# A two-layer hybrid attention trunk in fp32: the sparse values and their gate computed by channel instead of by token

## What is computed

```python
h = rms_norm(x, pre_w)
dq, dk, dv, dg, sq, sk, sv, sg, iq, ik, iw = split(h @ w_in)
oa = diff_attention(dq, dk, dv)              # 4 heads, value dim 128
oa = rms_norm(oa, subln_w) * (1 - lambda_init) * silu(dg)
score = relu(iq @ ik) . iw                   # index scores, 8 heads
idx = top_k(score, 64)                       # the 64 keys of each query
ob = softmax(sq @ sk[idx]) @ sv[idx]         # 4 heads of dim 128
ob = ob * silu(sg)
x = x + rms_norm(concat(oa, ob) @ w_out, post_w)
```

## Time and profile before

| | |
|---|---|
| median of 3 runs | 299.26 us |
| time of the profiled execution | 298.92 us |
| its span | 297.1 us |
| granted TensorE clock, mean | 0.996 |
| busy: PE / DVE / ACT / POOL | 97% / 79% / 55% / 25% |
| DMA: read, written | 56.06 MB, 6.82 MB |

### The profile page before, as it was taken

How to read it: one execution, slowest core, us unless ns; L and a number is a source line. 1 busy time by engine, 2 the same in 40 slices (tenths; PEclk the granted TensorE clock), 3 DMA queues, 4 the chain that set the end, 5 groups by cost and what they waited for, 6 DMA issues and landing times.

```text
span 297.1 us, 4373 instructions
## 1 busy us (share of the span) xinstructions
PE 289.3 (97%) x1544; PEld 243.8 (82%) x1544; DVE 234.4 (79%) x474; ACT 164.4 (55%) x284; POOL 74.9 (25%) x116
## 2 busy tenths in 40 slices
PE   8999999999999999899999999999999999999992
PEld 7799877788877888788888988778887788888892
DVE  4755789898978999867984686968898799999343
ACT  6988664635366775503676764473742948651101
POOL 6559410303305133001061740003302140210101
PEclk9999999999999999999999999999999999999998
DMA  7999959558755948994049796947768297476012
GB/s 251 369 365 394 387 214 317 195 130 251 189 194 91 336 143 216 225 290 138 1 146 377 236 358 144 393 164 195 231 128 284 47 272 262 142 137 147 0 71 71
DMA packets 77173, 63.15 MB, mean 213 GB/s; under 512 B 47200, under 2 KB 54112, under 8 KB 77152
## 3 DMA queue, kind: packets, MB, share of 16 engines
q1 hardware_dynamic: 76864, 62.62, 68.2%
q10 hardware_dynamic: 288, 0.26, 0.3%
HBM read 56.06 MB, written 6.82 MB: 212 GB/s over the span
## 4 chain that ended last, share of the span: by engine, by line
PE 85%; DVE 6%; DMA 3%; ACT 3%; issue 1%; SPq 1%; POOLq 0%; DVEq 0%; POOL 0%; ACTq 0%
PE bank_a L474 17%; PE bank_a L479 17%; PE bank_a L483 17%; PE bank_a L631 7%; PE bank_s L631 6%; PE bank_a L491 4%; PE bank_o L608 3%; ACT xt_pbuf L845 2%; DVE w_lo L1001 2%; PE bank_t L453 2%; DMA pT<-turned 1%; PE bank_s L572 1%; DMA turned<-dkT 1%; PE bank_o L757 1%; PE bank_s L584 1%
## 5 line engine op out<-in xcount | busy, mean ns | idle before, releaser
L1001 DVE TENSOR_TENSOR w_lo<-w_raw,w_hi 128x2048 fp32r<-128x2048 f32 (+1 forms) x46 | 99.4, 2168 | 17.2 <-ACT w_hi L774 16.9
L774 ACT ACTIVATE w_hi<-w_raw 128x2048 fp32r<-128x2048 f32 (+1 forms) x46 | 81.9, 1785 | 28.4 <-PE bank_a L483 19.7
L474 PE MATMUL bank_a<-w_hi,h_hi 128*128 128x512 f32 (+1 forms) x272 | 72.1, 387 | 0.0
L479 PE MATMUL bank_a<-w_hi,h_lo 128*128 128x512 f32 (+1 forms) x272 | 69.9, 378 | 0.0
L483 PE MATMUL bank_a<-w_lo,h_hi 128*128 128x512 f32 (+1 forms) x272 | 69.8, 378 | 0.0
L479 PEld LDWEIGHTS bank_a<-w_hi,h_lo 128*128 128x128 f32 x272 | 49.8, 188 | 9.6
L483 PEld LDWEIGHTS bank_a<-w_lo,h_hi 128*128 128x128 f32 x272 | 49.8, 188 | 9.5
L474 PEld LDWEIGHTS bank_a<-w_hi,h_hi 128*128 128x128 f32 x272 | 48.1, 188 | 10.5 <-issue 2.7
L1444 POOL TENSOR_TENSOR rt<-nat,tab 128x256 f32<-128x256 f32 x10 | 8.5, 854 | 103.6 <-ACT nat L829 103.6
L829 ACT ACTIVATE nat<-bank_a,st 128x512 f32<-128x512 f32 x20 | 13.6, 686 | 30.7 <-PE bank_a L483 30.7
L845 ACT ACTIVATE xt_pbuf<-xt_pbuf,st 128x128 f32<-128x128 f32 (+1 forms) x48 | 21.2, 443 | 14.5 <-DVE st L1150 14.5
(11 more groups left out here) (198 smaller groups left out, 426.3 us busy)
## 6 DMA issues: line engine op xcount, KB each, us to landing
w_raw<-in_w_in SPq DMA_DIRECT2D x30, 1024.0 KB, 6.6
w_raw<-in_w_out SPq DMA_DIRECT2D x8, 1024.0 KB, 5.7
w_raw<-in_w_in SPq DMA_DIRECT2D x8, 584.0 KB, 7.5
turned<-mixn SPq DMA_DIRECT2D x28, 128.0 KB, 2.7
prm<-in_rows SPq DMA_DIRECT2D x2, 705.0 KB, 7.7
w_raw<-in_w_in SPq DMA_DIRECT2D x2, 512.0 KB, 6.0
xres<-in_x SPq DMA_DIRECT2D x2, 512.0 KB, 9.4
dqT<-turned SPq DMA_DIRECT2D x2, 512.0 KB, 5.9
```

The source lines that it names most:

```text
L474: pe.matmul(bank, h_hi[:, HALF * half + kk, tok], whi[:, kk, :], start=half == 0 and kk == 0, stop=False)
L479: pe.matmul(bank, h_lo[:, HALF * half + kk, tok], whi[:, kk, :], start=False, stop=False)
L774: act.activation(unit(w_hi, u), unit(raw, u), ACT.Copy).then_inc(hi_done.sem, 1)
L1001: dve.tensor_tensor(unit(w_lo, u), unit(raw, u), unit(w_hi, u).bitcast(F32), ALU.subtract).then_inc(lo_done.sem, 1)
```

## The change

- **Gate (chunk SG).** `turned_gate` swaps the operands: a 128x128 tile of weights is stationary, the moving operand is `h` over all 256 tokens. A group is now two tiles of 128 channels by 256 tokens, 48 matmuls of 256 columns instead of 24 of 512. The gate stands by channel, and each token is a column.
- **Root per column.** `rx` can no longer be ACT's per-partition scale. SP writes it to DRAM (before unit 9's DMA) and reads it back as a row on all partitions (`rx_rows`, before unit 11's DMA). ACT's move is a plain copy. POOL multiplies the gate by `rx_rows` in two instructions of 128x512 ahead of the DQ rotary embedding, and ACT applies Silu in place, two instructions of 128x512 after split_hi(13).
- **Probabilities.** DVE's reciprocals move ahead (`invert(12)`, `invert(13)`, `invert(14)`), POOL multiplies the exponentials by 1/sum in `pbuf` (one 128x512 instruction for each use), and `turn_probs` waits for that (`normed`).
- **Order.** `invert(12)` stands where `turn_probs(PS0)` stood; this one moves behind the last choose and mask_unchosen. `invert(13)` and `invert(14)`, which wait for ACT's exponentials, stand between gate_diff(0) and split_lo(20).
- **Values.** values(2) and values(3) swap their operands too, so bank O holds channels by tokens. `gate_dsa` is now one multiplication of 128x512, a copy to `h_hi` and a subtraction to `h_lo`. The two turn_mix and the two drain_mix of the sparse half are gone.
- **SP.** The four puts of PS0 move ahead of the wait for split_lo(19) and of unit 23's DMA, and the get of PS0 goes ahead of the next unit's DMA.

```diff
+                    if u == 5:
+                        sp.wait_ge(rx_ready.sem, rx_ready.at(layer, 2))
+                        sp.dma_start(scratch[-1][0, :].rearrange("(p b) -> p b", p=P), rx).then_inc(rx_put.sem, 16)
+                    if u == 7:
+                        sp.wait_ge(rx_put.sem, rx_put.at(layer, 16))
+                        sp.dma_start(rx_rows[:, :], scratch[-1].to_broadcast([P, SEQ])).then_inc(rx_landed.sem, 16)
...
+                    if u == 19:
+                        put_probs(layer, PS0)
                     sp.wait_ge(lo_done.sem, lo_done.at(layer, u + 1))
                     sp.dma_start(unit(raw, u + RING), weights(layer, u + RING)).then_inc(raw_landed[u % RING].sem, 16)
...
                 for u in range(RING):
                     if u == 0:
-                        put_probs(layer, PS0)
+                        get_probs(layer, PS0)
                     if u == 1:
-                        get_probs(layer, PS0)
                         put_probs(layer, PS1)
...
+                    def products(w, x, first=False, last=False):
+                        for kk in range(HALF):
+                            for c in range(2):
+                                cols = slice((2 * pair + c) * P, (2 * pair + c + 1) * P)
+                                mm = pe.matmul(bank[:, c * SEQ:(c + 1) * SEQ], w[:, kk, cols], x[:, HALF * half + kk, :],
...
-                            mm = pe.matmul(O[o % 2][:, h * E:(h + 1) * E], part, v[:, t, h * E:(h + 1) * E],
+                            v_part = v[:, t, h * E:(h + 1) * E]
+                            still, moving = (part, v_part) if o < 2 else (v_part, part)
+                            mm = pe.matmul(O[o % 2][:, h * E:(h + 1) * E], still, moving,
...
-                turn_mix(T_MS0, 0, 2)
...
-                pe.wait_ge(t_drained.sem, t_drained.at(layer, T_MS0 + 1))
+                pe.wait_ge(sparse_split.sem, sparse_split.at(layer, 1))
                 out_part(1, 0, 0)
...
-                turn_mix(T_MS1, 1, 3)
...
+                def sparse_silu():
+                    for j in range(2):
+                        act.wait_ge(sg_scaled.sem, sg_scaled.at(layer, j + 1))
+                        act.activation(gate[:, j, 1, :], gate[:, j, 1, :], ACT.Silu).then_inc(sg_ready.sem, 1)
...
+                def invert(use):
+                    r, n_rows = 4 * (use % 4), 4 if use == 12 else 2
+                    dve.wait_ge(exps_done.sem, exps_done.at(layer, use + 1 - S_DIFF0))
+                    dve.reciprocal(inv[:, r:r + n_rows], sums[:, r:r + n_rows]).then_inc(inverted.sem, 1)
+
                 def turn_probs(n, use):
-                    dve.wait_ge(exps_done.sem, exps_done.at(layer, use + 1 - S_DIFF0))
+                    dve.wait_ge(normed.sem, normed.at(layer, use + 1 - S_DSA0))
...
                 def gate_dsa(b):
+                    dve.wait_ge(sg_ready.sem, sg_ready.at(layer, 2))
                     dve.wait_ge(o_filled.sem, o_filled.at(layer, 3 + b))
-                    gated(2 + b, [inv[:, (h if b == 0 else 4 * (1 + h // 2) + h % 2):][:, 0:1] for h in range(HEADS)])
+                    tok = slice(b * P, (b + 1) * P)
+                    dve.tensor_tensor(mixn[:, b, :].rearrange("p (j c t) -> p j c t", c=2, t=P),
+                                      O[b][:, :].rearrange("p (j c t) -> p j c t", c=2, t=P),
+                                      sparse_gate[:, :, :, tok], ALU.mult).then_inc(mixn_ready.sem, 1)
+                    dve.wait_ge(mixn_ready.sem, mixn_ready.at(layer, 3 + b))
+                    mix = mixn[:, b, :].rearrange("p (k t) -> p k t", k=HALF)
+                    link(dve.tensor_copy(h_hi[:, 0:HALF, tok], mix))
+                    dve.tensor_tensor(h_lo[:, 0:HALF, tok], mix, h_hi[:, 0:HALF, tok].bitcast(F32),
+                                      ALU.subtract).then_inc(sparse_split.sem, 1)
...
                 choose(1, 2)
-                turn_probs(PS0, 12)
+                invert(12)
                 choose(1, 1)
                 mask_unchosen(1)
+                turn_probs(PS0, 12)
                 split_lo(layer, 19)
...
                 gate_diff(0)
+                invert(13)
+                invert(14)
                 split_lo(layer, 20)
                 turn_probs(PS1, 14)
...
                 gate_dsa(0)
                 split_lo(layer, 22)
-                drain_mix(T_MS0, h_hi, h_lo, 0)
                 split_lo(layer, 23)
                 split_mix()
                 gate_dsa(1)
                 weight_y(0)
                 residual(0)
-                drain_mix(T_MS1, h_hi, h_lo, 1)
...
                 for b in range(BLOCKS):
+                    for use in ((12,), (13, 14))[b]:
+                        n_rows, n, r = (4, P, 4 * (use % 4)) if b == 0 else (2, SEQ, 4 * (use % 4))
+                        pool.wait_ge(inverted.sem, inverted.at(layer, use + 1 - S_DSA0))
+                        probs = pbuf[:, use % 4, :].rearrange("p (h n) -> p h n", n=n)
+                        pool.tensor_tensor(probs, probs, inv[:, r:r + n_rows][:, :, None].to_broadcast([P, n_rows, n]),
+                                           ALU.mult).then_inc(normed.sem, 1)
                     pool.wait_ge(o_squared.sem, o_squared.at(layer, b + 1))
```

More of the change, by code:

```diff
@@ L89 @@
 T_IK, T_PD0, T_PD1A, T_SK, T_PD1B = 4, 5, 6, 7, 9
-T_MD0, T_MS0, T_MS1 = 10, 11, 12
-T_USES = 13
+T_MD0 = 10
+T_USES = 11
 DKS, PS0, MD1S, PS1 = range(3, 7)
@@ L156, in build_trunk @@
         trig = sb("trig", [P, 8, BLOCKS * NF])
+        rx_rows = sb("rx_rows", [P, SEQ])
+        sparse_gate = gate[:, :, 1, :].rearrange("p j (c t) -> p j c t", t=SEQ)
         pos_f = sb("pos_f", [P, BLOCKS])
@@ L247, in build_trunk @@
         mix_split = count("mix_split", 1)
+        rx_put, rx_landed = count("rx_put", 16), count("rx_landed", 16)
+        sg_scaled, sg_ready = count("sg_scaled", 2), count("sg_ready", 2)
+        inverted = count("inverted", 3)
+        normed, sparse_split = count("normed", 3), count("sparse_split", BLOCKS)
         subln_ready = count("subln_ready", 1)
@@ L460, in turn_nat, with turned_gate @@
                         turn(j + n, [nat[:, slot, b, f * P:(f + 1) * P] for f in (2 * n, 2 * n + 1) for b in range(BLOCKS)])
+                def turned_gate(layer, bank, u, pair, half):
+                    def products(w, x, first=False, last=False):
[3 more added lines that the diff above has]
+                                mm = pe.matmul(bank[:, c * SEQ:(c + 1) * SEQ], w[:, kk, cols], x[:, HALF * half + kk, :],
+                                               start=first and half == 0 and kk == 0 and c == 0,
+                                               stop=last and half == 1 and kk == HALF - 1 and c == 1)
+                        return mm
+                    if layer:
+                        pe.wait_ge(h_hi_done.sem, h_hi_done.at(layer, 2 + half + 1))
+                    pe.wait_ge(hi_done.sem, hi_done.at(layer, u + 1))
+                    products(unit(w_hi, u), h_hi, first=True)
+                    if layer:
+                        pe.wait_ge(h_lo_done.sem, h_lo_done.at(layer, 2 + half + 1))
+                    products(unit(w_hi, u), h_lo)
+                    pe.wait_ge(lo_done.sem, lo_done.at(layer, u + 1))
+                    return products(unit(w_lo, u), h_hi, last=True)
                 def part_of(g, half):
@@ L468, in part_of @@
                     whi, wlo = unit(w_hi, u), unit(w_lo, u)
+                    if chunk == SG:
+                        return turned_gate(layer, bank, u, b, half)
                     if layer:
@@ L744, in body @@
                 out_part(0, 1, 0).then_inc(out_unit_used.sem, 1)
-                turn_mix(T_MS1, 1, 3)
                 out_part(0, 1, 1).then_inc(out_unit_used.sem, 1)
-                pe.wait_ge(t_drained.sem, t_drained.at(layer, T_MS1 + 1))
+                pe.wait_ge(sparse_split.sem, sparse_split.at(layer, 2))
                 out_part(1, 1, 0).then_inc(out_unit_used.sem, 1)
@@ L827, in move @@
                         act.wait_ge(dk_squares.sem, dk_squares.at(layer, 1))
+                    if chunk == SG:
+                        act.activation(dst, bank[:, 0:WIDTH], ACT.Copy).then_inc(proj_moved.sem, 1)
+                        return
                     root = {DQ: rd, SQ: rs}.get(chunk, rx)
-                    act.activation(dst, bank[:, 0:WIDTHS[chunk]], ACT.Silu if chunk in (DG, SG) else ACT.Copy,
+                    act.activation(dst, bank[:, 0:WIDTHS[chunk]], ACT.Silu if chunk == DG else ACT.Copy,
                                    scale=root[:, b:b + 1]).then_inc(proj_moved.sem, 1)
+                def sparse_silu():
+                    for j in range(2):
+                        act.wait_ge(sg_scaled.sem, sg_scaled.at(layer, j + 1))
+                        act.activation(gate[:, j, 1, :], gate[:, j, 1, :], ACT.Silu).then_inc(sg_ready.sem, 1)
                 def relu(j):
@@ L912, in body @@
                 split_hi(layer, 13)
+                sparse_silu()
```

(9 more changed lines are left out.)

4 lines of the change are left out of this document (removed).

## The result

The changed kernel takes 301.44 us (median of 7 runs, 300.29 to 301.96) against 299.26 us for the kernel before, run beside it: ratio 1.0056, 95% interval 1.004 to 1.0072. That is slower, by little, and 0.3 us above the 301.1 us predicted. The seven times lie in two groups, three at 300.3 to 300.4 and four at 301.4 to 302.0. The median falls in the upper one, so it shows 2.2 us of loss where the means (301.10 for 299.38) and the ratio show 1.7. The profiled execution (301.7 us, span 299.9 us for 297.1 before) is of the upper one too: its span is 2.8 us longer.

A forecast was written before the change was run, and what follows sets the result against it. PE, busy 97%, was taken as the bound, with DVE close behind. Gate +1.3 us, removed turns -1.8 and DVE's lag, as 2L - 4.4 with L 3.1, gave +1.8 us: 301.1 us, range 297.5 to 303.8.

The forecast's parts named there:

- Gate by channel: Gate matmuls on PE: 48 of 256 columns replace 24 of 512, +0.32 us for each of four groups, +1.3 us.
- that rival: Gate on PE: weight loads set the matmuls' pace, +8.6 us instead of +1.3, 308.4 us; chance 0.03.
- Turns removed: Sparse half on PE: four turns of 0.46 us each go, two per layer, -1.8 us.
- Price of one scaling: POOL's 128x512 multiplication of probabilities by 1/sum: 1.30 us, by the slope from 128 and 256 elements; bounds 0.69 and 2.1.
- Exclusion: POOL and DVE shut each other out: whichever is second waits, so split_lo(20) blocks POOL's scaling of use 14.
- The rival without exclusion: Uses 13 and 14 are scaled beside split_lo(20): lag 1.2 us, PE never waits, -1.6 us, 297.7 us; chance 0.20.
- Lag of 3.1 us: DVE's order in the sparse half: gate_diff(1) starts at 264.4 for 261.27 in layer 1, behind blocked scalings and POOL's root instructions.
- the cheaper scaling: POOL's scaling takes 0.8 to 1.0 us: lag 1.9 to 2.5, within 0.6 us of 299.3 us; chance 0.12.
- the likeliest case: Blocked exchange of POOL and DVE: lag 2.6 to 3.8 us, +0.8 to +3.2 us, 300.1 to 302.5; chance 0.55.
- From the lag to PE: PE waits for DVE before the out_parts: net +0.9 us in layer 1, -0.45 us in layer 0, with turns removed.
- the formula: Whole kernel's change for DVE lag L: 1.3 + (L - 1.7 - 0.46) + (L - 3.1 - 0.46) = 2L - 4.4.
- I take all this at nothing: Root's put and get on SP, POOL's gate scaling and ACT's Silu: covered by slack, two SP issues of 0.7 us at most.

The follow-up runs named there:

- the four kernels alike up to there: The changed kernel (301.44 us), and it with the root's put and get in layer 1 removed (300.15), only the get later (301.61), or both later (300.41).
- the trip left out: Changed kernel without the put and get of the root in layer 1, whose gate uses layer 0's roots: 300.15 us, ratio 1.0026.
- ACT's scaling alone: Changed kernel with uses 13 and 14 scaled by ACT, in four 128x256 instructions behind square_o(1), instead of POOL: 298.83 us, ratio 0.9987.
- the trip's move: Changed kernel with layer 1's root write at unit 9 and broadcast at unit 11, behind the index query's fetch: 300.41 us, ratio 1.0038.
- the order of the queue alone: Kernel before with only SP's new order, PS0's puts and get moved ahead: 298.94 us, ratio 0.9986.

## Why the prediction was right, step by step

**Gate by channel, +1.3 us.** Right. 0.119 us a matmul; the gate's stretch is 0.63 us longer in each layer, 1.27 in all. PE's weight loads did not bind, so that rival is out.

**Turns removed, -1.8 us.** Right in what it did at the end of layer 1. With block 1's scalings off POOL the rest of the profile is 102.01 to 102.59 us in four kernels. Without the wait before the sparse scores it is 102.01 to 102.07 in all four, for 102.97 before, which has no such wait. That is 0.90 to 0.96 us less, where two turns were put at 0.92.

**Price of one scaling, 1.30 us.** Too high: 1.04. The scaling of the gate, whose second operand is a full row, did take 1.31 us, so the slope from rows of 128 and 256 elements was good for such an instruction. What the trace before could not show is that with one number per partition and block as second operand it is cheaper. A sentence from the Trainium skill beside it ("GPSIMD Engine Reference", Elementwise — side-by-side cycle accounting): about 2.6 cycles an element for two inputs, an estimated 1.11 us for 512 elements at 1.2 GHz; the runs show 1.31 and 1.04 around that.

**Exclusion.** Right, and shown from three sides: 4.09 us for two scalings with split_lo(20) between them, 2.04 without it, and no stretching with the work on ACT. The rival without exclusion is out.

**Lag of 3.1 us.** Gate_diff(1) is 4.64 us later than before. Of these, 2.08 are PE's lateness from the gate and the index scores (values(2) starts at 267.71 for 265.63), which leaves 2.56 us. The missing 0.5 is two scalings at 0.26 less. With that the measured lag falls between two of the rivals: just above the cheaper scaling's 1.9 to 2.5 (chance 0.12) and just under the likeliest case's 2.6 to 3.8 (0.55).

**From the lag to PE.** Right in place, and in part in size. PE waits for DVE before out_part(0,0,0) in layer 1 (0.50 for 1.2 predicted) and before out_part(1,0,0) (0.54 and 0.50 for 0.7). In layer 1 the formula with a lag of 2.56 gives +0.4 us, and from the scores on the profile is +0.47. Up to the index scores of layer 1, their wait left out, the profile is +0.66 us for the +0.85 of both gates and layer 0's end, but the four kernels alike up to there show +0.66 to +1.37. The formula's sum of +1.8 was thus measured as 0.66 + 0.47 = **+1.1 us** in this profile; the two kernels that have the wait before the index scores taken away stand 0.9 and 1.0 us above the kernel before in their medians. By its own formula a lag of 2.56 gives +0.7. Taking block 1's scalings off POOL gives back some 1.2 us of layer 1's rest (a mean of 103.5 in five kernels that have them in the change's place, 102.3 in four without); what they cost in layer 0 can't be told from its spread of 1.2 us.

**The step that failed: "I take all this at nothing"**, of the root's put and get. Their two issues were priced (0.5 and 0.9 us measured), and nothing else. The write of 1 KB in 128 pieces landed only after 7.6 us in layer 1 (10.1 in layer 0), and what was queued behind it went slowly: the index query's puts took 9.70 us for 4.61. Its price is 1.64 us in this profile (0.45 to 1.64 in the eight that have it there). In the times it is 0.9 us by the ratios with the trip left out (1.0056 to 1.0026), and 0.5 with it moved (to 1.0038), where the intervals overlap; by the medians 1.0 to 1.3. A rule of the Trainium skill speaks for a slow write ("DMA: Bandwidth & Descriptors", Specifications): below 512 bytes a transfer does not reach line rate. That rule is about the small transfer itself, and it does not single this one out: from 160 to 190 us the kernel before moved 4288 packets under 512 bytes, with its puts at 4.61 us. That the transfers behind the 8-byte pieces suffer is shown by these runs alone.

By the prediction's own signs this was the miss: it said that it would be wrong if PE waited elsewhere, named the index key and values(3), and PE waited at the index scores. Its first sign came up too: the first scaling was to take 1.3 us and took 1.04.

So the total came out right, 301.44 for 301.1, from a lag term 0.7 us too large and a transfer term that was 0.5 to 1.6 us too small. That the two cancel to 0.3 us is luck. The prediction's mechanism is the larger part of the loss: ACT's scaling alone takes the ratio from 1.0056 to 0.9987. The two repairs add up as far as the intervals tell: ACT's scaling gains 0.69% and the trip's move 0.18%, which would give 0.9969, and both together measured 0.9974 (0.9958 to 0.9989).

## What to carry to other kernels

Price a small DMA by what stands behind it in its queue, not by its issue: a 1 KB write of 8-byte pieces cost 0.5 to 1.3 us, not far from the 1.3 us of matmul time that the change added, and PE's wait was gone with the write behind the transfers that somebody waits for. An elementwise instruction on GpSimd that meets VectorE's large ones was better off on ScalarE, which had the time (55% busy): the same two products took 1.71 us there and held nobody up. Compare single profiles with care: places in layer 0 differ by up to 1.2 us between executions of the same code. And when idle time before a wait is counted as a gain, look first whether the engine that waits is always that early: of 1.05 us counted here, the order of the queue alone brought 0.3 to 0.4.

## What the runs showed of the hardware

- GpSimd multiplies 128x512 by one number per partition and block in 1.04 us, and by a full second operand in 1.31 us. On VectorE the first takes 0.69 us.
- Two of these GpSimd instructions and a 128x2048 subtraction on VectorE hold each other up (4.09 us for 2.04, 2.83 for 2.28). Four ScalarE instructions of 128x256 beside the same subtraction do not (1.71 us, and 2.27 for the subtraction). Small VectorE instructions are held too: a copy of 128 elements took 1.22 us for 0.23 beside a GpSimd instruction of 1.29.
- A new stationary tile for every matmul of 256 columns, as the new gate has it, stays hidden: 0.119 us a pair.
- Behind a write of 128 pieces of 8 bytes on SP's queue the 16 DMA engines moved 100 to 221 GB/s from 170 to 175 us in the eight kernels that have it there, in place of 378 to 390 in the five that don't; in single microseconds 18 to 33. In two of them, looked at by the microsecond, the DMA share in the profile was 1.0 to 2.1 first and 0.1 to 0.6 later. Why, and whether larger pieces would cure it, was not tried.
- A fetch of 512 KB of turned queries landed 3.7 to 6.8 us after its issue before the sparse scores, and PE's wait there followed it (0 to 1.22 us).
- After 2.14 us of idle the granted clock was 0.57 over the next 4 us, with two quartets of 512 columns 1.78 and 1.71 us long from start to start: the lower level of 1.2 GHz, then the upper again. After the wait of 1.64 us in the changed kernel the granted clock stayed at 1.00, and the next quartets kept their usual pace.
